# Retention heads of a hybrid DiT kernel: gate, norm sums, decay tables and weight splits reordered

## The reference, cut to what matters

```python
q, k, v, gate = split(hn @ w_in)           # q, k rotated; k scaled by 256 ** -0.5
k_c, v_c = split(gn @ w_in[:, hdk:2*hdk+hdv])
s_fwd = retention_state(k_c, v_c, log_g[0], (l - 1) - pos)
s_bwd = retention_state(k_c, v_c, log_g[1], pos)
o = retention_scan(q, k, v, log_g[0], s_fwd, strict=False) \
  + flip(retention_scan(flip(q), flip(k), flip(v), log_g[1], s_bwd, strict=True))
mu = mean(o, -1); var = mean((o - mu) ** 2, -1)
y = (o - mu) * rsqrt(var + EPS) * gn_gain * silu(gate)
out = y @ w_o
```

## Time and profile before

| what | before |
|---|---|
| median of 3 runs (lowest to highest) | 3266.49 us (3265.23 to 3267.14) |
| the profiled execution | 3265.89 us |
| its span | 3264.2 us, 42549 instructions |
| PE busy | 3095.1 us (95%) |
| DVE busy | 1833.8 us (56%) |
| ACT busy | 866.4 us (27%) |
| granted clock, mean | 0.982 |
| chain that ended last | PE 89%, DVE 6%, ACT 3% |

### The profile page before, as it was taken

One profiled execution on the slowest core, in us unless ns is written; L12 is line 12 of the kernel. 1 busy time (PEld: TensorE's weight loads), 2 busy tenths in 40 slices (PEclk: granted clock), 3 DMA queues, 4 the chain that ended last, 5 costly groups with the idle time before them and its releaser, 6 DMA issues.

```text
span 3264.2 us, 42549 instructions
## 1 busy us (share of the span) xinstructions
PE 3095.1 (95%) x17560; PEld 2655.0 (81%) x17560; DVE 1833.8 (56%) x2670; ACT 866.4 (27%) x1188; POOL 36.7 (1%) x73
## 2 busy tenths in 40 slices
PE   6999999879999999999999999999799999989999
PEld 4888888767777788888888888888678787778887
DVE  4765565645655576655664455567454636464444
ACT  3211111433443431111132111113222223242221
POOL 0000000000000000000000000000000000000000
PEclk8999999989999999999999999999899999999999
DMA  6333232110111043323221232231111111122222
GB/s 236 131 130 112 90 116 90 46 39 27 51 39 39 27 155 116 116 99 107 103 90 55 75 116 103 90 116 54 62 56 51 67 47 65 43 74 97 96 91 89
DMA packets 40977, 277.72 MB, mean 85 GB/s; under 512 B 4352, under 2 KB 5632, under 8 KB 8000
## 3 DMA queue, kind: packets, MB, share of 16 engines
q1 hardware_dynamic: 31024, 205.85, 17.9%
q0 software_dynamic: 9872, 70.72, 6.1%
HBM read 274.45 MB, written 2.10 MB: 85 GB/s over the span
## 4 chain that ended last, share of the span: by engine, by line
PE 89%; DVE 6%; ACT 3%; issue 1%; DMA 1%; SPq 0%; DVEq 0%; POOL 0%; ACTq 0%
PE ps L299 29%; PE ps L301 28%; PE ps L300 28%; PE ps L613 2%; PE ps L327 1%; DVE wl L1212 1%; ACT wh L856 1%; DVE act_buf L1296 1%; DVE xnl L1300 1%; PE ps L313 0%; DMA ada_w<-ada 0%; DVE nrm L1507 0%; ACT xnh L887 0%; PE ps L345 0%; PE ps L412 0%
## 5 line engine op out<-in xcount | busy, mean ns | idle before, releaser
L299 PE MATMUL ps<-xnh,wl 128*128 128x512 f32 (+1 forms) x3040 | 1063.4, 350 | 35.6 <-DVE wl L1212 14.8
L300 PE MATMUL ps<-xnl,wh 128*128 128x512 f32 (+1 forms) x3040 | 1053.9, 347 | 0.0
L301 PE MATMUL ps<-xnh,wh 128*128 128x512 f32 (+1 forms) x3040 | 1052.8, 346 | 0.0
L299 PEld LDWEIGHTS ps<-xnh,wl 128*128 128x128 f32 x3040 | 582.3, 192 | 118.1 <-DVE xnl L1300 16.5
L301 PEld LDWEIGHTS ps<-xnh,wh 128*128 128x128 f32 x3040 | 582.4, 192 | 70.0
L300 PEld LDWEIGHTS ps<-xnl,wh 128*128 128x128 f32 x3040 | 582.8, 192 | 68.1 <-issue 1.0
L856 ACT ACTIVATE wh<-raw 128x2048 fp32r<-128x2048 f32 (+1 forms) x178 | 332.7, 1871 | 607.1 <-PE ps L301 607.1
L1212 DVE TENSOR_TENSOR wl<-raw,wh 128x2048 fp32r<-128x2048 f32 (+1 forms) x183 | 410.2, 2242 | 112.8 <-ACT wh L856 112.6
L1354 DVE SCALAR_TENSOR_TENSOR h<-ps,coef,h 128x512 f32<-128x512 f32 x624 | 371.9, 642 | 129.9 <-PE ps L301 129.5
L301 PE MATMUL ps<-hidh,wh 128*128 128x512 f32 (+1 forms) x1232 | 429.3, 348 | 0.0
L299 PE MATMUL ps<-hidh,wl 128*128 128x512 f32 (+1 forms) x1232 | 425.7, 346 | 3.1 <-DVE h L1312 3.1
(11 more groups left out here) (226 smaller groups left out, 3090.4 us busy)
## 6 DMA issues: line engine op xcount, KB each, us to landing
raw<-weights SPq DMA_DIRECT2D x183, 1024.0 KB, 4.8
adaw<-ada POOLq DMA_DIRECT2D x64, 1024.0 KB, 5.1
ada_w<-ada SPq DMA_DIRECT2D x8, 1024.0 KB, 20.4
h<-x_in SPq DMA_DIRECT2D x1, 2048.0 KB, 9.0
c_act<-c_rows POOLq DMA_DIRECT2D x2, 1024.0 KB, 5.1
out<-h SPq DMA_DIRECT2D x8, 256.0 KB, 2.0
h<-x_in SPq DMA_DIRECT2D x1, 1024.0 KB, 28.3
cs<-rope_mla POOLq DMA_DIRECT2D x1, 512.0 KB, 3.4
```

The lines of the kernel that those rows point to most:

```text
L299: mm(dst, lhs[1][rows], rhs[0][rows], start=first, stop=False)
L300: mm(dst, lhs[0][rows], rhs[1][rows], start=False, stop=False)
L301: return mm(dst, lhs[0][rows], rhs[0][rows], start=False, stop=last)
```

## The change

- POOL loads `cr` and `dist` when DVE has used the last of the modulation weights, not after the last norm.
- Decay tables: `dec_lat` is the minimum of two products (forward log decay by distance, backward by distance), two DVE instructions; ACT computes the two terms of `dec_ctx` from `dist` with scale and bias per partition, one into the new tile `far`. Two more constants in `lg` hold the biases. The DVE instructions stand after the split of q, the Exps after ACT's high parts of q, and the addition of the two terms after `split_lo(s1)`, ahead of the first values.
- DVE's first `split_lo(s0)` of a head stands ahead of q's rotation.
- PE waits for the last values pairs later: before `outputs(0)` instead of before the scores; the first half of gate 0 (k 0 to 3) goes ahead of the wait for `outputs(1)`.
- The gates use banks 0, 3, 4, 5. Each centring signals by itself; PE waits for one before gate 2 and a second before gate 3. The squares go to `rrs`, `rt` 0, `rt` 1, `rt` 0; DVE adds two of them to the first, and PE adds the fourth with a second group of sums. The sums stand after a quarter of gate 2, the spread after three quarters.
- ACT loads the Sqrt table ahead of the squares. `split_hi(s0)` and `split_lo(s0)` of the gating stand before the first Silu and the first slice; those of s1 after the last slice and the third `y` addition. The Silus alternate between two buffers and run one slice ahead; DVE makes a slice's low part after the next slice's product.
- At the end of a head PE no longer waits for the last additions; the next head waits for all but two before q and for all before k.

```diff
+G_BANKS = (0, 3, 4, 5)
@@ pool
-            pool.wait_ge(xn_ready, c.next(xn_ready, 4 * KD))
+            pool.wait_ge(ada_used, c.next(ada_used, 2))
@@ tensor, head
                 pe.wait_ge(w_ready[s0], c.next(w_ready[s0]))
+                if not first:
+                    pe.wait_ge(y_added, c.ahead(y_added, -2))
...
                 pe.wait_ge(w_ready[s1], c.next(w_ready[s1]))
+                if not first:
+                    pe.wait_ge(y_added, c.ahead(y_added, 0))
...
                 values(s0, 6, 2)
-                pe.wait_ge(v_ready, c.next(v_ready, 2))
...
                 pe.wait_ge(sc_ready, c.next(sc_ready, 3))
+                pe.wait_ge(v_ready, c.next(v_ready, 2))
                 outputs(0)
                 values(s1, 3, 1)
                 pe.wait_ge(v_ready, c.next(v_ready))
                 values(s1, 2, 2)
...
+                pe.wait_ge(w_ready[s0], c.next(w_ready[s0]))
+                gate(0, s0, range(0, 4))
                 pe.wait_ge(v_ready, c.next(v_ready, 2))
                 outputs(1)
-                pe.wait_ge(w_ready[s0], c.next(w_ready[s0]))
-                gate(0, s0, 2)
+                gate(0, s0, range(4, KD))
                 pe.wait_ge(osum_ready, c.next(osum_ready))
-                mm(ps[:, 0, :], ones[:, 0:1].to_broadcast([P, P]), rrs[:], start=True, stop=True).then_inc(mu_full, 1)
-                gate(1, s0, 3)
-                pe.wait_ge(vsq_added, c.next(vsq_added, 4))
-                quarter_sums(1, 0, rrs, S).then_inc(var_full, 1)
+                mm(ps[:, 1, :], ones[:, 0:1].to_broadcast([P, P]), rrs[:], start=True, stop=True).then_inc(mu_full, 1)
+                gate(1, s0, range(KD))
                 pe.wait_ge(w_ready[s1], c.next(w_ready[s1]))
                 pe.wait_ge(cen_done, c.next(cen_done))
-                gate(2, s1, 4)
+                gate(2, s1, range(0, 2))
+                pe.wait_ge(vsq_added, c.next(vsq_added, 2))
+                quarter_sums(1, 0, rrs, S, True, False)
+                pe.wait_ge(vsq_done, c.next(vsq_done, 4))
+                quarter_sums(1, 0, rt[:, 0, :], S, False, True).then_inc(var_full, 1)
+                gate(2, s1, range(2, 6))
                 pe.wait_ge(rms_ready, c.next(rms_ready))
                 spread((1, None), rrs, S).then_inc(rms_full, 1)
-                gate(3, s1, 5)
+                gate(2, s1, range(6, KD))
+                pe.wait_ge(cen_done, c.next(cen_done))
+                c.next(cen_done, 2)
+                gate(3, s1, range(KD))
...
                 if not last:
-                    pe.wait_ge(y_added, c.next(y_added, 3))
+                    c.next(y_added, 3)
@@ scalar, head
-                act.wait_ge(dec_done, c.next(dec_done))
-                fn(dec_lat, dec_lat, ACT.Exp)
-                fn(dec_ctx, dec_ctx, ACT.Exp)
-                fn(rt_flat[:, 0:640], rt_flat[:, 0:640], ACT.Exp).then_inc(dec_exp, 1)
                 act.wait_ge(qk_full, c.next(qk_full))
                 split_hi(s0)
                 for j in range(2):
                     part(qk_val, qk_hi, rq[:, 0, j, :], rt[:, j, :])
+                act.wait_ge(dec_done, c.next(dec_done))
+                fn(dec_lat, dec_lat, ACT.Exp)
+                fn(dec_ctx, dist[:, L:DIST_W], ACT.Exp, bias=lg[:, 5, at(i)], scale=lgf)
+                fn(far[:], dist[:, L:DIST_W], ACT.Exp, bias=lg[:, 6, at(i + RET_HEADS)], scale=nlgb).then_inc(dec_exp, 1)
                 act.wait_ge(qk_full, c.next(qk_full))
                 split_hi(s1)
...
-                act.wait_ge(cen_done, c.next(cen_done))
+                sqrt_table()
                 for j in range(4):
-                    if j >= 2:
+                    act.wait_ge(cen_done, c.next(cen_done))
+                    if j == 3:
                         act.wait_ge(vsq_added, c.next(vsq_added))
-                    fn(rt[:, j % 2, :], dec[:, j, :], ACT.Square).then_inc(vsq_done, 1)
+                    fn(rt[:, (j - 1) % 2, :] if j else rrs[:], dec[:, j, :], ACT.Square).then_inc(vsq_done, 1)
...
+                act.wait_ge(g_full, c.next(g_full, 2))
+                split_hi(s0)
+                silu(0)
                 for j in range(4):
-                    act.wait_ge(g_full, c.next(g_full))
-                    fn(rt[:, 2, :], ps[:, 2 + j, :], ACT.Silu).then_inc(g_silu, 1)
-                    if j in (1, 3):
-                        split_hi((s0, s1)[j // 2])
+                    if j + 1 < 4:
+                        silu(j + 1)
                     part(g_val, g_hi, st[:, 0, j, :], dec[:, j, :])
+                split_hi(s1)
@@ vector, head
-                ts(dec_lat, dist[:], 0.0, lgf, ALU.max, ALU.mult)
-                step(ts(rt_flat[:, 0:DIST_W], dist[:], 0.0, nlgb, ALU.min, ALU.mult))
-                step(tt(dec_lat, dec_lat, rt_flat[:, 0:DIST_W], ALU.add))
-                ts(dec_ctx, dist[:, 256:DIST_W], float(L), lgf, ALU.add, ALU.mult)
-                ts(rt_flat[:, 0:640], dist[:, 256:DIST_W], -float(S), nlgb, ALU.add, ALU.mult).then_inc(dec_done, 1)
-                dve.wait_ge(dec_exp, c.next(dec_exp))
-                step(tt(dec_ctx, dec_ctx, rt_flat[:, 0:640], ALU.add))
                 dve.wait_ge(qk_full, c.next(qk_full))
+                split_lo(s0)
                 rotate(0)
...
-                split_lo(s0)
+                step(ts(dec_lat, dist[:], nlgb, None, ALU.mult))
+                stt(out=dec_lat, in0=dist[:], scalar=lgf, in1=dec_lat, op0=ALU.mult, op1=ALU.min).then_inc(dec_done, 1)
...
                 split_lo(s1)
+                dve.wait_ge(dec_exp, c.next(dec_exp))
+                step(tt(dec_ctx, dec_ctx, far[:], ALU.add))
...
                 for j in range(4):
-                    ins = tt(dec[:, j, :], ps[:, 4 + j, :], rt[:, 2, :], ALU.add)
-                ins.then_inc(cen_done, 1)
-                for j in range(4):
-                    dve.wait_ge(vsq_done, c.next(vsq_done))
-                    if j == 0:
-                        nc.vector.tensor_copy(rrs[:], rt[:, 0, :]).then_inc(vsq_added, 1)
-                    else:
+                    tt(dec[:, j, :], ps[:, 4 + j, :], rt[:, 2, :], ALU.add).then_inc(cen_done, 1)
+                for j in (1, 2):
+                    dve.wait_ge(vsq_done, c.next(vsq_done, 2 if j == 1 else 1))
+                    if j == 2:
                         dve.wait_ge(vsq_added, c.next(vsq_added))
-                        tt(rrs[:], rrs[:], rt[:, j % 2, :], ALU.add).then_inc(vsq_added, 1)
+                    tt(rrs[:], rrs[:], rt[:, j - 1, :], ALU.add).then_inc(vsq_added, 1)
...
                 nc.vector.reciprocal(rrs[:, 0:P], rrs[:, 0:P]).then_inc(rms_ready, 1)
+                split_lo(s0)
...
                 for n_y in range(KD if last else 2 * KD):
                     add_y(n_y % KD, 1, n_y)
+                    if n_y == 2:
+                        split_lo(s1)
```

More of the change, by code:

```diff
@@ L1145, in part, with at, head @@
                 fn(dst, src, ACT.Copy).then_inc(done, 1)
-            def head(last=False):
-                act.wait_ge(dec_done, c.next(dec_done))
-                fn(dec_lat, dec_lat, ACT.Exp)
-                fn(dec_ctx, dec_ctx, ACT.Exp)
-                fn(rt_flat[:, 0:640], rt_flat[:, 0:640], ACT.Exp).then_inc(dec_exp, 1)
+            def at(n):
+                return slice(n, n + 1) if isinstance(n, int) else bass.ds(n, 1)
+            def head(i, last=False):
+                lgf, nlgb = lg[:, 1, at(i)], lg[:, 2, at(i + RET_HEADS)]
                 act.wait_ge(qk_full, c.next(qk_full))
@@ L1193, in head @@
                 split_hi(s1)
[L1195 to L1199 removed]
+            head(0)
+            with c.loop(act, RET_HEADS - 2, {dec_done: 1, qk_full: 2, qk_val: 4, v_full: 6, sc_val: 6, o_full: 4, cen_done: 4,
+                                             vsq_added: 2, var_full: 1, g_full: 4, g_val: 4, y_full: 16,
+                                             raw_full[0]: 64, raw_full[1]: 64}) as i:
+                head(i + 1)
             c.next(y_added, 2 * KD * (RET_HEADS - 1))
[L1201 removed]
+            head(RET_HEADS - 1, last=True)
             ffn(1, slot, last=True)
```

63 lines of the change are left out of this document (33 added, 30 removed).

## The result

| | before | after |
|---|---|---|
| median of 4 runs each (lowest to highest) | 3266.16 us (3265.23 to 3267.14) | 3219.14 us (3218.74 to 3219.99) |
| ratio, 95% interval | | 0.9856 [0.9839, 0.9873] |
| profiled execution, its span | 3265.89, 3264.2 us | 3219.45, 3217.5 us |
| PE busy | 3095.1 us (95%) | 3081.1 us (96%) |
| granted clock, mean | 0.982 | 0.986 |

The change makes the kernel 47.0 us faster; 44.8 were forecast. The first view is again what PE waited for over the four heads (total, times, longest), against the earlier trace rows.

What follows compares the result with a forecast made beforehand. PE bounds the heads, losing only idle time and low clock. Gains 18.9 + 16.75 + 5.4 - 2.5 + 0.5 + 5.7 = 44.75 us take 3265.89 to 3221.1, median 3221.7; range 3214 to 3237, the forecast's own 3218 to 3226.

Steps and rivals of the forecast that it cites:

- Gate half and v_ready: Before the second outputs: half of gate 0 there removes PE's wait of 1.6 us; 0.4 arises before the mean's matmul.
- Centring and squares: Before the sums of squares: separate centring signals and PE summing the last square remove 1.5 us; extra small matmuls add 0.36.
- Splits out of gating: Before the first `y`: wait of 2.2 us goes, 0.3 spare; from the last values' end (T), 37.85 becomes 33.0.
- The y block: `y` blocks of heads 0 to 2 and next head's start: waits gone, clock 1.0, 22.4 us each, 16.75 gained.
- rival B: Clock stays low for the same stretches (10.2 us) or gating chain 1 to 2 us late per head; 3226 to 3236, chance 0.20.
- Head 3's block and last stage: Head 3's `y` block to the last stage's wait: 5.4 us gained; a wait of 3.0 behind `split_lo(s0)` stays.
- Decay tables: Before scores: table work hidden behind k with 2.6 us spare, but the addition before the first values costs 2.5 in all.
- Scores: Wait of 1.65 us before the scores goes but 1.4 returns at the fifth; 0.5 gained over three heads.
- First head: Values start 15.3 us earlier, PE idles 9.4 before the third; net 5.7 gained after a low-clock stretch of 1.7.
- C: DVE's score-stage queue is later, 12 us over four heads, and the first head's 5.7 is lost; 3239.4, chance 0.09.
- D: Slower: ACT's wait for `dec_done` before `split_hi(s1)` delays k copies, k rotation and PE's third value; 3275, chance 0.03.
- E: Head 0 keeps its clock and the last stage's clock stays up: 2 to 6 us more, 3216 to 3219, chance 0.07.

Runs made afterwards that it cites:

- head-end wait: The changed kernel with PE's wait for the last three additions to `h` put back at each head's end; 3224.04 us, ratio 0.987.
- the delay: The changed kernel with eight useless DVE instructions of 640 columns ahead of slice 0 in every head; 3244.51 us, ratio 0.9926.
- the two waits: The changed kernel with the gating's s0 split behind slice 0 and six useless DVE instructions between the two additions of squares; 3240.84 us, ratio 0.9921.
- first-head kernel: The changed kernel with the `dec_ctx` addition later and, in head 0, the first values split early (ACT before Exps, DVE before k); 3210.69 us.
- last split moved: The changed kernel with addition later, s0 split behind scores, early first values, and the last head's `split_lo(s0)` behind the last stage's first norm; 3201.16 us.

## Why the prediction was right

The forecast was 3221.7 us, the median is 3219.14, inside the forecast's own range (3218 to 3226). By its steps:

- **Gate half and v_ready.** Right. The wait of 1.6 went and one on the mean came, 0.20 for the 0.4 that I had. The kernel with gate 0 whole shows both by themselves.
- **Centring and squares.** The wait before the sums is gone. I had the sums end 22.6 behind T (2545.6 less 2523.0); they start 21.95 behind it (2528.38 less 2506.43) and take 0.42: 22.4.
- **Splits out of gating.** T to the first `y` 33.14 for 33.0. The tightest place had 0.5 to spare for the 0.3 forecast, and putting the splits back costs 1.5 to 1.8 a head. The spare is real and small: a delay of 4.2 us on DVE brought 3.5 to 3.8 of waiting.
- **The y block.** 22.4 at granted clock 1.00, as forecast; the waits for `h` went, and the kernel with the head-end wait prices those at the head's start at 1.5 each; those inside the block are read from the rows alone. The low clock went with the idle time. This was rival B, and the runs bear on it twice: the idle places that stayed (0.96, 1.36 and 0.20 for 0.85, 1.4 and 0.4) left the clock up, and of the waits put back before `y` those of 3.5 to 3.8 brought it down in all heads, those of 1.5 to 1.8 in none. The Trainium skill's rule ("TensorE: Matmul & The Clock Gate", What's actually happening), by which the gate follows how busy PE has been, agrees with these rows.
- **Head 3's block and last stage.** 5.37 for 5.4; the wait of 3.0 that I said would stay is 2.8.
- **Decay tables.** Hidden but for the addition, as said; its wait is 0.96 for 0.9 to 1.0, and moving it alone gives back 3.2 in four heads. In head 0 the prediction had it in the first head's chain, and there it is 0.8 of the 9.5 (8.7 without it). The minimum of two products took 1.15, in my range of 0.7 to 1.5, where I took 1.09. I expected 2.2 for three Exps and they take 2.6 (from 2447.79 to 2450.37 in head 1), as two of them now read scale and bias from a table; with 2.6 to spare this was not seen.
- **Scores.** The wait came back as 1.36 for 1.4; I had a net gain of 0.17 a head from it; from the wait of 1.49 to 1.36 it is 0.13. The split ahead of the scores was its cause, as the kernel with it moved shows.
- **First head.** Idle 9.53 for 9.4, net gain 5.3 (44.83 less 39.54 to the end of the third values) for 5.7. The low stretch behind the idle time was there as expected, 4.2 us of it over work, so 2.1 instead of 1.7.
- **The sum.** 43.6 us of the change in the profiled executions for 44.75. The gain there is 1.1 below the forecast, 0.4 of it in the first head; the rest is spread over terms of a few tenths. The median is 2.6 below the forecast all the same. Of the profiled difference 2.5 us lie ahead of the stage and 0.5 behind it, where the same code measured twice differs by as much. The median also lies 0.3 below the profiled execution where the forecast had it 0.6 above. The same kernel measured again came to 3224.67, 3.0 above the forecast. So the steps hold to about 1 us; on which side of the forecast the total came out, and that it isn't further off, is luck.
- **What no run isolates.** The half gate (4.95), the head's end (4.3), the split of slot s0 (7.6) and the early tables (3.8) were put back one at a time: 20.7 of the 43.6 us. The gain before the sums (1.33 a head), the waits for `h` inside the blocks (1.84 to 1.92 a head) and the low stretches of the blocks (six before, none now) are read from the rows before and after. Why the first two went is argued from the order of DVE's queue and not shown by a run; that idle time ahead of `y` can bring the third is shown.
- **Rivals C, D and E.** C and D gave nothing: the waits in the score stage were 0.96 and 1.36, not 1.5 more each, and no wait on the Exps is in the list. The median lies beside E's 3216 to 3219, but not for E's reason, since head 0 kept its low stretch. By the drain of 1.38 us that the Trainium skill ("ScalarE: Activation LUTs", What ACT_TABLE_LOAD costs) adds to a table load, PE's first `y` would by estimate have come 0.5 later; here the rows disagree with the page, because the load ends at 2532.56 and the Silu starts at 2532.57.

## What to carry to other kernels

Follow one period of the bound engine from one anchor to the next and write down at each wait which queue released it and what stood ahead of the releasing instruction: the splits, additions and Exps at the front of DVE's and ACT's queues cost the 7.6 us of slot s0's split and most of the 18 us that were left, while the half gate and the head's end were won in PE's own order. Price a moved block twice, once where it leaves and once where it arrives: the addition was hidden where it had been and cost its full wait where the change put it. Look too at what a removed wait had covered: the split ahead of the scores didn't move, and its wait showed as soon as the one before it was gone. A wait of 2 us on TensorE can cost 3.7, because a low stretch of 3.4 us can come with it; in these heads waits of 1.8 and less, one at a time, brought none, so a long wait is worth shortening even where it can't be removed.

## What the runs showed of the hardware

**The return of the loop cost 3 us in some executions.** Heads 1 and 2 are two rounds of one loop. In the profiled executions of three kernels (the delay, the two waits, the first head) PE waits 3.0 to 3.2 us at the start of head 2 for nothing but "issue", as in the row at 2578.53 above; in the others it doesn't. Instruction packets then run through head 2; the two stand together in the traces, and no run tests that one causes the other. The instruction queue from 2565 to 2700 us (packets, MB, share of 16 engines), in the first-head kernel and in the changed one:

```profile
q8 instruction: 6, 0.10, 0.3%
```

```profile
q8 instruction: 1, 0.02, 0.0%
```

In the first-head kernel that round lasts 140.7 us instead of 136.0, 4.7 more, which is about the distance of this execution (3215.43, its slowest) from its median (3210.69). The profiled execution with the delay (3252.53) is likewise its slowest, 8.0 above its median; that with two waits isn't slow among its own. Two other kernels (gate whole, last split moved) have one execution 8.3 and 6.2 us above the median that wasn't the profiled one, so whether it has this cause is open. Why these packets run in some executions and not in others, these runs don't tell.

**Scale and bias from a table cost ACT time.** An Exp of 640 columns took 0.72 us with neither (721 ns on average, eight of them in the kernel before) and takes 0.91 with both as columns of `lg` (L1171 above). The Trainium skill ("ScalarE: Activation LUTs", What ACT_TABLE_LOAD costs) gives 93 ns for each such operand, by estimate 0.19 for two: the rows agree.

**The same code's low stretches move.** Before and behind the heads they cost 2 to 3 us more or less from one execution to the next, as the repeat showed. A change of that size has to be read from its own stretch of the trace.
